# A two-block transformer kernel on one core: another order inside linear attention, and six small modulation blocks spread over a feed-forward layer

## The reference, cut to what matters

```
sh1, sc1, g1, sh2, sc2, g2 = split(silu(cond) @ w_ada[i] + b_ada[i], 6)   # per layer i
q, k, v, r = split(h @ w_in)                       # 4 heads, dk 128, dv 256
z = (h @ w1) @ w2 + b ;  g = log_sigmoid(z) / 16   # forward and backward gates
b = cumsum(g) in chunks of 64 tokens
q_dec = q * exp(b);  k_intra = k * exp(-b);  k_state = k * exp(b_last - b)
scores = where(mask, q_dec @ k_intra.T, 0);  o_intra = scores @ v
o = q_dec @ S;  S = S * exp(b_last) + k_state.T @ v      # from chunk to chunk
u = depthwise_conv3(h @ w_up);  a, g = split(u);  out = (silu(g) * a) @ w_down
```

## Time and profile before

| | us |
|---|---|
| three runs | 4405.87, 4408.59 (median), 4409.0 |
| profiled execution, its own time | 4407.32 |
| profiled execution, span of the core | 4405.5 |
| TensorE busy | 4093.7 (93%) |
| TensorE weight loads | 2999.4 (68%) |
| VectorE busy | 1901.5 (43%) |
| ScalarE busy | 1346.8 (31%) |

### The profile page before, as it was taken

One profiled execution on the slowest core, in us unless ns is written; L12 is line 12 of the kernel. 1 busy time (PEld: TensorE's weight loads), 2 busy tenths in 40 slices (PEclk: granted clock), 3 DMA queues, 4 the chain that ended last, 5 costly groups with the idle time before them and its releaser, 6 DMA issues.

```text
span 4405.5 us, 47227 instructions
## 1 busy us (share of the span) xinstructions
PE 4093.7 (93%) x19208; PEld 2999.4 (68%) x19208; DVE 1901.5 (43%) x3004; ACT 1346.8 (31%) x2255; POOL 16.9 (0%) x33
## 2 busy tenths in 40 slices
PE   6989999999988899999888999899988889998999
PEld 3656578888765557887665665588866665656887
DVE  1333245554443326554674521433437654223434
ACT  2222132322144424332234431422223334223222
POOL 0000000000000000000000000000000000000000
PEclk8889999999999999998999999999989999999999
DMA  4232134232310013332211122233222111222331
GB/s 154 67 105 66 40 95 118 89 110 89 103 40 23 22 44 91 96 93 78 78 49 48 39 86 74 70 94 103 78 89 63 48 46 58 66 87 72 96 96 62
DMA packets 385173, 333.48 MB, mean 76 GB/s; under 512 B 12416, under 2 KB 351872, under 8 KB 384832
## 3 DMA queue, kind: packets, MB, share of 16 engines
q1 hardware_dynamic: 382384, 319.09, 24.0%
q0 software_dynamic: 2576, 11.37, 0.8%
HBM read 328.34 MB, written 2.10 MB: 75 GB/s over the span
## 4 chain that ended last, share of the span: by engine, by line
PE 74%; DVE 7%; ACT 5%; issue 2%; DMA 0%; ACTq 0%; DVEq 0%
PE ps L400 54%; PE ps L411 3%; PE ps L413 3%; PE ps L412 3%; PE ps L532 2%; DVE WL L362 1%; ACT WH L354 1%; PE ps L2061 1%; ACT arena_m L1726 1%; PE ps L1686 1%; PE ps L2039 1%; PE ps L601 1%; DVE arena_m L1708 1%; PE ps L602 1%; PE ps L603 1%
## 5 line engine op out<-in xcount | busy, mean ns | idle before, releaser
L362 DVE TENSOR_TENSOR WL<-ring,WH 128x2048 fp32r<-128x2048 f32 (+3 forms) x221 | 461.3, 2088 | 357.0 <-ACT WH L354 356.7
L354 ACT CAST WH<-ring 128x2048 fp32r<-128x2048 f32 (+3 forms) x221 | 384.0, 1738 | 477.0 <-PE ps L400 386.9
L400 PE MATMUL ps<-MH,WH 128*128 128x512 f32 x1024 | 399.8, 390 | 3.2 <-DVE WL L362 3.2
L400 PE MATMUL ps<-ML,WH 128*128 128x512 f32 x1024 | 399.5, 390 | 0.0
L400 PE MATMUL ps<-MH,WL 128*128 128x512 f32 x1024 | 399.4, 390 | 0.0
L411 PE MATMUL ps<-MH,WH 128*128 128x512 f32 x768 | 344.0, 448 | 13.1 <-DVE WL L362 13.1
L400 PE MATMUL ps<-IH,WH 128*128 128x512 f32 (+1 forms) x880 | 337.4, 383 | 0.0
L400 PE MATMUL ps<-IL,WH 128*128 128x512 f32 (+1 forms) x880 | 326.2, 371 | 0.0
L400 PE MATMUL ps<-IH,WL 128*128 128x512 f32 (+1 forms) x880 | 325.5, 370 | 0.0
L413 PE MATMUL ps<-MH,WL 128*128 128x512 f32 x768 | 310.3, 404 | 0.0
L412 PE MATMUL ps<-ML,WH 128*128 128x512 f32 x768 | 309.7, 403 | 0.0
(11 more groups left out here) (291 smaller groups left out, 6689.3 us busy)
## 6 DMA issues: line engine op xcount, KB each, us to landing
ring<-in_w_in SPq DMA_DIRECT2D x62, 1024.0 KB, 5.2
ring<-in_w_ada SPq DMA_DIRECT2D x48, 1024.0 KB, 8.2
ring<-in_ffn_w_up SPq DMA_DIRECT2D x88, 512.0 KB, 5.2
ring<-in_w_gu SPq DMA_DIRECT2D x88, 512.0 KB, 5.2
ring<-in_ffn_w_down SPq DMA_DIRECT2D x28, 768.0 KB, 4.5
ring<-in_w_down SPq DMA_DIRECT2D x28, 768.0 KB, 4.3
ring<-in_gla_w_in SPq DMA_DIRECT2D x8, 1024.0 KB, 9.7
ring<-in_gla_w_out SPq DMA_DIRECT2D x8, 1024.0 KB, 4.9
```

The costliest lines, as they stand in the source:

```text
L354: nc.scalar.copy(split_slot(key, WH), raw_slot(key)).then_inc(act_done, mark("act", ("rounded", k)))
L362: nc.vector.tensor_tensor(split_slot(key, WL), raw_slot(key), split_slot(key, WH).bitcast(F32), ALU.subtract).then_inc(dve_done, mark("dve ...
L400: m = nc.tensor.matmul(out, l, r, start=(i == 0), stop=(i == len(pairs) - 1))
```

## The change

In linear attention the gate matmuls are cut by token group, not given out all at once: `g` 1 (512 tokens, both directions) at the start of step 0, then q of the 512 tokens, and `g` 0 (context, both directions) at the end of the step. `abs` and `min` follow by token group. `soft` of direction 0 comes after q is copied. In ACT's lists E1, E2 and E3 stand ahead of the copies of k and v that they shared a step with; the first modulation block moves from step 3 to step 2 and each v tile behind it one place back. The ring's list has that block's two pieces ahead of the v weights. Among the four output matmuls on the states the last two change places, so that the halves of the array's columns are 0, 1, 0, 1 and not 0, 1, 1, 0.

In `a0` the second layer's blocks come after j = 0, 2, 4, 5, 7, 9, 11, 12, 14, 16, 18, 19, and each is turned after the next j.

```diff
+        ADA1 = [0, 2, 4, 5, 7, 9, 11, 12, 14, 16, 18, 19]
...
+                ada(0, 4 + 2 * h)
                 piece((("gla_in", h), 1), [(0, cols(g_in, 1024 + h * 256, 1280 + h * 256))])
-                ada(0, 4 + 2 * h)
                 ada(0, 5 + 2 * h)
...
-            def ada1(c):
-                ada(1, c)
-                if c == FT // 2 - 1:
-                    ada(1, c + 1)
+            def ada1(j):
+                if j in ADA1:
+                    ada(1, ADA1.index(j))
...
-        PROJ_PE = [[("g", 0), ("q", 1)], [("q", 0), ("k", 1)], [("k", 0), ("v", 0), ("v", 1)],
+        PROJ_PE = [[("g", 1), ("q", 1), ("g", 0)], [("q", 0), ("k", 1)], [("k", 0), ("ada", 0), ("v", 0)],
...
             elif what == "g":
                 nc.tensor.wait_ge(act_done, at(("zs",)))
-                for t0, tn in ALL:
-                    for d in range(2):
+                t0, tn = ALL[i]
+                for d in range(2):
...
             elif what == "abs":
-                for t0, tn in ALL:
-                    nc.scalar.wait_ge(pe_done, at(("g", h, i, t0)))
+                t0, tn = ALL[i]
+                for d in range(2):
...
+                    nc.scalar.wait_ge(pe_done, at(("g", h, d, t0)))
...
-                for t0, tn in ALL:
-                    nc.vector.wait_ge(act_done, at(("abs", h, i)))
+                t0, tn = ALL[i]
+                nc.vector.wait_ge(act_done, at(("abs_part", h, i)))
+                for d in range(2):
...
             for i in range(2):
-                for d in range(2):
+                for d in (0, 1) if i == 0 else (1, 0):
                     t = TILES[d][s]
                     c = i if d == 0 else 1 - i
...
-                if j % 2:
-                    extra(j // 2)
+                extra(j)
...
+        def ada1_pe(j):
+            if j in ADA1:
+                ada_pe(1, ADA1.index(j))
+            if j - 1 in ADA1:
+                ada_turn_pe(1, ADA1.index(j - 1))
```

More of the change, by code:

```diff
@@ L857, in build @@
         LAST = (GLA_C - 1, 0)
-        PROJ_PE = [[("g", 0), ("q", 1)], [("q", 0), ("k", 1)], [("k", 0), ("v", 0), ("v", 1)],
-                   [("v", 2), ("v", 3), ("ada", 0)], [("v", 4), ("v", 5), ("ada", 1)], [("kt", 0), ("kt", 1), ("turn", 0)]]
+        PROJ_PE = [[("g", 1), ("q", 1), ("g", 0)], [("q", 0), ("k", 1)], [("k", 0), ("ada", 0), ("v", 0)],
+                   [("v", 1), ("v", 2), ("v", 3)], [("v", 4), ("v", 5), ("ada", 1)], [("kt", 0), ("kt", 1), ("turn", 0)]]
         def proj_pe(h, what, i):
@@ L896, in proj_pe @@
                     m.then_inc(pe_done, mark("pe", ("kt", h, i, half)))
-        PROJ_ACT = [[("abs", 0), ("abs", 1), ("soft", 0), ("q", 1)], [("soft", 1), ("q", 0), ("k", 1), ("E1", 0)],
-                    [("k", 0), ("E1", 1), ("E2", 0), ("v", 0), ("v", 1)], [("v", 2), ("v", 3), ("E2", 1), ("E3", 0), ("ada", 0)],
-                    [("v", 4), ("v", 5), ("E3", 1), ("ada", 1)], [("kt", 0), ("kt", 1)]]
+        PROJ_ACT = [[("abs", 1), ("q", 1), ("abs", 0), ("soft", 0)], [("soft", 1), ("q", 0), ("k", 1), ("E1", 0)],
+                    [("E1", 1), ("k", 0), ("ada", 0), ("E2", 0), ("v", 0)], [("E2", 1), ("E3", 0), ("v", 1), ("v", 2), ("v", 3)],
+                    [("E3", 1), ("v", 4), ("v", 5), ("ada", 1)], [("kt", 0), ("kt", 1)]]
         def proj_act(h, what, i):
@@ L914, in proj_act @@
             elif what == "abs":
-                if h:
-                    nc.scalar.wait_ge(pe_done, at(("kt", h - 1, i, 1)))
-                for t0, tn in ALL:
-                    nc.scalar.wait_ge(pe_done, at(("g", h, i, t0)))
-                    nc.scalar.activation(gb["E", i][:, t0:t0 + tn], bank_of(("g", h, i, t0))[:, 0:tn], ACT.Abs,
-                                         bias=v("gate_b", 4 * i + h)).then_inc(
-                                             act_done, mark("act", ("abs", h, i), ("free", ("g", h, i, t0))))
+                t0, tn = ALL[i]
+                for d in range(2):
+                    if h:
+                        nc.scalar.wait_ge(pe_done, at(("kt", h - 1, d, 1)))
+                    nc.scalar.wait_ge(pe_done, at(("g", h, d, t0)))
+                    nc.scalar.activation(gb["E", d][:, t0:t0 + tn], bank_of(("g", h, d, t0))[:, 0:tn], ACT.Abs,
+                                         bias=v("gate_b", 4 * d + h)).then_inc(
+                                             act_done, mark("act", ("abs", h, d), ("abs_part", h, i), ("free", ("g", h, d, t0))))
             elif what == "soft":
@@ L953, in proj_act @@
                                        act_done, mark("act", ("KT", h, i), ("free", ("kt", h, i, half))))
-        PROJ_DVE = [[("min", 0), ("min", 1), ("B", 0)], [("B", 1), ("QD", 0)], [("QD", 1), ("KI", 0)],
+        PROJ_DVE = [[("min", 1), ("min", 0), ("B", 0)], [("B", 1), ("QD", 0)], [("QD", 1), ("KI", 0)],
                     [("KI", 1), ("KS", 0)], [("KS", 1)], [("ada", 0), ("ada", 1)]]
@@ L963, in proj_dve @@
                     nc.vector.wait_ge(pe_done, at(("o", h - 2, 5)))
-                for t0, tn in ALL:
-                    nc.vector.wait_ge(act_done, at(("abs", h, i)))
-                    nc.vector.tensor_scalar(gb["KI", i, p][:, t0:t0 + tn], bank_of(("g", h, i, t0))[:, 0:tn],
-                                            v("gate_b", 4 * i + h), 0.0, ALU.add, ALU.min).then_inc(
-                                                dve_done, mark("dve", ("minz", h, i), ("free", ("g", h, i, t0))))
+                t0, tn = ALL[i]
+                nc.vector.wait_ge(act_done, at(("abs_part", h, i)))
+                for d in range(2):
+                    nc.vector.tensor_scalar(gb["KI", d, p][:, t0:t0 + tn], bank_of(("g", h, d, t0))[:, 0:tn],
+                                            v("gate_b", 4 * d + h), 0.0, ALU.add, ALU.min).then_inc(
+                                                dve_done, mark("dve", ("minz", h, d), ("free", ("g", h, d, t0))))
             elif what == "B":
```

33 lines of the change are left out of this document (10 added, 23 removed).

## The result

The changed kernel takes 4326.57 us (median of 4 runs, 4325.66 to 4329.4) against 4407.23 us for the kernel before, timed with it (4 runs, 4404.28 to 4409.0): a ratio of 0.9819, 95% interval 0.9802 to 0.9836, or 80.7 us less. Forecast were 4336 us, in a range of 4324 to 4357.

What follows compares the result with a forecast made beforehand. PE was taken as the bound, so only its idle time and lower clock could be won: 58.2 us in linear attention plus 16.0 in `a0` less 1.6, 72.6 off 4407.3, plus 1.3 to the median: 4336 us, range 4324 to 4357.

Steps and rivals of the forecast that it cites:

- Gates by token group: Linear attention, head 0's projections and three hand-overs: all eight PE waits for `min` go, 14.1 us, with no new wait.
- The clock behind the waits: Lower PE clock behind the gate waits goes: 15.3 us at three hand-overs, 2.5 us in head 0's q and k.
- exponents: Steps 3 and 4: six state-update waits go, 10.1 us, plus 3.0 in matmuls behind them and 4.7 of lower clock.
- pieces: Modulation pieces ahead of v weights: four PE waits for their DMA go, 6.3 us, plus 2.2 of lower clock.
- The clock that may still fall: Small matmuls at the hand-overs may lower PE's clock: one fall taken, 1.6 us lost; bounds none to 4.8 us.
- The end of `a0`: Behind the last up tiles: spreading the blocks removes PE's waits and lower clock, 16.0 us.
- rival 3: End of `a0`: the last j's convolution holds PE, not the ring; stall stays, 16 us back, 4352; chance 0.06.
- Rival 5: Inside `a0`: spread blocks hold ring slots and stall PE, 16 us each; four stalls make it slower, 4416; chance 0.04.
- The column halves: State output matmuls in alternating halves: taken as 0; up to 10 us lost or 2.4 us gained thought possible.
- Rival 4: Linear attention: state-update waits stay because KI itself holds DVE's updates; 18 us back, 4354; chance 0.06.

Runs made afterwards that it cites:

- gates-only kernel: The kernel before with only gates, abs and min cut by token group: 4374.41 us, ratio 0.9931.
- kernel with the old gates: The changed kernel with gates, abs and min by direction again: 4365.65 us, ratio 0.9907.
- kernel with the turnings apart: The changed kernel with a head's two block turnings moved apart, to steps 3 and 5: 4330.82 us, ratio 0.983; run again, 4327.36 us, ratio 0.9824.
- spread alone: The kernel before with only the second layer's blocks spread evenly over `a0`: 4384.44 us, ratio 0.9955.
- v-copies kernel: The changed kernel with ACT's exponents behind the k and v copies again, matrix engine order as changed: 4357.88 us, ratio 0.9894.
- attention alone: The changed kernel with the second layer's blocks in `a0` back at their old places: 4344.47 us, ratio 0.9864.
- halves back: The changed kernel with output matmuls on the states in the old column order 0, 1, 1, 0: 4325.68 us, ratio 0.9829.
- one block: The kernel before with one modulation block, not two, after the last j of `a0`, turned at once: 4392.7 us, ratio 0.9972.
- v weights first: The changed kernel with the ring's list in old order, v weights ahead of both modulation blocks: 4351.32 us, ratio 0.988.
- halves alone: The kernel before with only the output matmuls' column halves in turn, 0, 1, 0, 1: 4406.06 us, ratio 1.0.

## Why the prediction was right, point by point

**Gates by token group (14.1 us of waits): right.** All eight waits are gone in the gates-only kernel too. The chain that was to be late next was worked out at 10.5 us, with 1 us more where a head has one before it, against 13.5 us of PE work. In head 1 of the changed kernel the context tiles end at 222.01 (221.31 and 0.70) and the updates of step 1 start at 231.81; DVE has done the first two at about 232.63 (half of 1.63 later), and PE comes to them at 235.03. DVE's updates, then PE's tiles and outputs, each from its engine's timeline:

```profile
231.81 1.63 DVE L1069 SCALAR_TENSOR_TENSOR arena_a<-arena_a,ps 128x256 f32<-128x256 f32 x4
```

```profile
221.31 0.70 PE L399 MATMUL ps<-arena_a 16*128 16x256 f32 x4
...
235.03 1.08 PE L1035 MATMUL ps<-arena_a,under 128*64 128x256 f32 x8
```

10.6 us of chain, 13.0 of cover, a margin of 2.4 where 2 to 3 was forecast.

**The clock behind the waits (15.3 + 2.5), exponents (17.8) and pieces (8.5): right, and each a little small.** A head from turning to turning was 88.75 us before and is 72.10 where no fall is left: 16.65 us, where the terms give 15.4 (3.74 of gate waits, 5.1 of clock, 3.4 + 1.0 + 1.57 for the exponents, 0.64 for the piece). By the kernel with the old gates the split is 9.5 for the gates, of which 5.8 the clock for my 5.1, and 7.15 (88.75 less 81.60) for exponents and pieces, for my 6.6. Over three heads that is 3.7 us too little. Head 0's projections gave 13.3 us for about 12. The forecast called this clock "behind the waits". That holds for how long it stays low (13.6 us in head 1 with the waits, 6.8 without), but not for what starts the fall: it comes 0.6 us ahead of the wait at the end of head 0's projections in the kernel with the old gates, and it still comes in two of three places with no wait at all.

**The clock that may still fall (1.6 us): this step failed in size.** The forecast put one fall at 1.6 us, with 4.8 as the outer bound. There are two, and each costs 3.3 us (75.38 from turning to turning in head 1, 75.36 in head 0, 72.10 in head 2), 6.5 together; the kernel with the turnings apart puts both at 7.1, of which 0.4 lie ahead of the first. Two of the forecast's own signs came out against it: q is at 7.1 us in one of the three hand-overs only, and the clock is at 0.50 for 6.8 us at the other two, where beyond 3 us was to mean wrong. The price was taken from the stretch around 208 to 211 us, where the lower clock lasted for one group; here it takes the gates, the state products and part of q. The error doesn't show in the sum, as the terms above are too small by about as much: forecast 58.2 less 1.6, 56.6 us; measured 63.2 (13.3 and three times 16.65) less 6.5, 56.7. That the two errors cancel to 0.1 us is luck.

That it can fall with PE busy was right, but the row that was read for it does not show it: in windows of 0.1 us the clock of before falls at about 235.3, 0.2 us after the wait has begun at 235.12, and ahead of head 0 at about 146.6, where PE is busy up to 146.65. In the changed kernel it is plain. The windows at 136 and 212 us have PE busy for 2.00 of 2.00 us at 0.50, and the same work in another order keeps 1.00. The Trainium skill (TensorE: Matmul & The Clock Gate, "What's actually happening") says "activity releases the throttle"; with that read as "busy", the trace does not agree.

**The end of `a0` (16.0 us): right.** 16.3 in the changed kernel and in the one with the spread alone. One block behind the last j in place of two takes the 7.09 us wait away and has the `w_down` piece rounded in time, so the cause was the slot of the ring (against rival 3). Rival 5, stalls inside `a0`, did not come: the stretch that the earlier trace rows shows with 479.84 us of 480 is now, in the changed kernel's windows

```profile
600.00:1080.00 480.00, 480.00 (x3016) 414.92 (x3016) 238.19 (x325) 137.74 (x158) 0.00 (x0) 1.00 0.35 105
```

**The column halves (0): right.** The feared loss, a wait for the later of two updates, shows in the old kernel as 0.4 us more a wait, but the matmuls behind it are shorter by as much. The 3.0 us counted behind these waits fit: from the first of the eight to the block it was 3.75 us before, with 2.13 of wait, and is 1.01 in the changed kernel (258.27 to 259.28), which leaves 0.6 for the 0.5 counted each time.

**Rival 4**, in which the waits for updates stay, fell with the v-copies kernel: ACT's order alone brings all six back.

**From 4336 to 4326.6.** The profiled executions differ by 77.9 us where 72.6 were forecast. The 5.3 us between lie outside of what the change touches: 1.7 in the output projection, 1.5 from the end of `a0` to the first rope load and 3.0 up to the second, then 1.8 lost up to the third and 0.4 gained behind it, make 4.9 before rounding; 0.1 and 0.3 are the two sums above. Nothing there was edited. The other 4.1 us are how profiled executions stand to medians: the forecast added 1.3; after, the median is 2.8 below. Apart from the 0.4 us of the two sums, no term of the forecast stands for these 9.4 us.

## What to carry to other kernels

An in-order engine that copies tiles out of PSUM holds whatever stands behind the copy: put work whose data is ready (here the exponents) ahead of copies that must wait for a matmul, and cut groups that need more banks than there are, so that the tiles come when banks are free. A wait of the matrix engine can cost much more than its length when the clock is low with it: in this kernel 9.5 us for 3.74 at the gates, 16.3 for 10.5 at the end of `a0`, 17.5 for 12.4 with the copies first. The last piece of a ring of weights should reuse a slot that was read a whole tile earlier. When the waits are gone, look for the clock in a tile whose length is known; and judge a change of a few us by landmarks around it, not by the whole time.

## What the runs showed of the hardware that was not expected

**The clock falls on small matmuls without a wait.** 9.14 and 8.85 us for a q tile that takes 7.13, behind 16 matmuls of 128x2, scores and 16-row gates, with PE never idle; 7.13 three times when eight of the 128x2 matmuls are moved to step 3 and the other eight ahead of the last transposes. How often it happens and for how long varies: the linear attention alone, with the same code there, had one such tile, at 7.74 us.

**The same code downstream takes 777 or 785 us.** Between the first and the second rope load (latent attention and the next feed-forward layer, edited in no kernel here) the kernels take:

| kernel | us |
|---|---|
| changed; spread alone; turnings apart; halves back; one block | 777.18; 777.31; 776.95; 777.52; 777.57 |
| before; attention alone | 780.15; 780.17 |
| gates alone; v copies first; v weights first; old gates; halves alone | 784.74; 784.87; 785.10; 784.93; 784.87 |

The second traces of the changed kernel and of the turnings apart gave 777.12 and 776.87. Nothing in the edits orders them so. Of the 7.7 us between the changed kernel and the one with v copies first, 6.6 are busy time of PE on the same matmuls (731.29 and 737.89 us over the stretch), at a mean granted clock of 0.98 and 0.97. In aligned stretches of 50 us, 150 us behind the load, the changed kernel and the one with v copies first have about the same PE busy time and different clocks. The changed kernel:

```profile
1339.40:1389.40 50.00, 45.31 (x216) 29.37 (x212) 15.63 (x26) 21.60 (x46) 0.00 (x0) 0.97 0.07 24
```

And v copies first:

```profile
1360.20:1410.20 50.00, 45.59 (x214) 29.21 (x211) 14.00 (x24) 20.40 (x44) 0.00 (x0) 0.93 0.05 16
```

What decides it was not found. It is the largest part of what made 17.5 us in linear attention come out as 31 in the whole time of one experiment, and it means that, of this kernel, a difference of under about 8 us in one profiled execution can be the clock's.
